# Reordering the opening of a two-layer diffusion trunk: x1 of the fourth token tile, the split of the MLP's first weight unit, and two modulation loads

## The reference

```python
sh_m, sc_m, gt_m, sh_f, sc_f, gt_f = jnp.split((silu_c @ ada_w[i] + ada_b[i])[:, None, :], 6, axis=-1)
h = modulate(rms_norm(x, norm_g[i, 0]), sh_m, sc_m)          # h * (1 + scale) + shift
y = pool_mixer(h, pool_w[j], pool_scale[j])                   # four groups of 256 channels, windows 2, 4, 8, 16
x = x + gt_m * rms_norm(y, norm_g[i, 1])                      # this is x1 below
hf = modulate(rms_norm(x, norm_g[i, 2]), sh_f, sc_f)
x = x + gt_f * rms_norm(jnp.square(jax.nn.relu(hf @ ffn_w1[i])) @ ffn_w2[i], norm_g[i, 3])
```

## Time and profile before

| | us |
|---|---|
| median of three runs | 937.25 |
| lowest, highest | 936.25, 937.87 |
| the profiled execution | 937.82 |
| its span in the profile | 935.8 |
| PE busy in the span | 915.7 |
| ACT busy, DVE busy | 430.9, 648.2 |

### The profile page before, as it was taken

How to read it: one execution, slowest core, us unless ns; L and a number is a source line. 1 busy time by engine, 2 the same in 40 slices (tenths; PEclk the granted TensorE clock), 3 DMA queues, 4 the chain that set the end, 5 groups by cost and what they waited for, 6 DMA issues and landing times.

```text
span 935.8 us, 11417 instructions
## 1 busy us (share of the span) xinstructions
PE 915.7 (98%) x4623; PEld 755.0 (81%) x4623; DVE 648.2 (69%) x625; ACT 430.9 (46%) x523; POOL 48.9 (5%) x80
## 2 busy tenths in 40 slices
PE   8889999999999999999999999999999999999996
PEld 6658888888888888889888888898888888888885
DVE  5696297589678866686667644857857873793688
ACT  6564484454246333264222224555534634543554
POOL 3002110010001001000101000000000000000000
PEclk8999999999999999999999999999999999999998
DMA  9999889527734586324656531183870662175134
GB/s 303 321 352 347 232 221 313 213 74 187 285 114 125 174 314 222 116 76 170 211 179 209 188 124 49 62 298 102 258 260 21 180 202 80 54 217 165 37 68 179
DMA packets 91403, 170.86 MB, mean 183 GB/s; under 512 B 4270, under 2 KB 34066, under 8 KB 91352
## 3 DMA queue, kind: packets, MB, share of 16 engines
q1 hardware_dynamic: 83912, 155.25, 48.5%
q0 software_dynamic: 7440, 14.89, 8.2%
HBM read 163.81 MB, written 6.32 MB: 182 GB/s over the span
## 4 chain that ended last, share of the span: by engine, by line
PE 52%; DVE 2%; issue 1%; ACT 0%; DVEq 0%
PE ps L674 17%; PE ps L676 17%; PE ps L675 17%; PE ps L768 1%; DVE y L1945 0%; DVE y L1580 0%; DVE in_lo L1591 0%; PE ps L703 0%; DVE xs L1956 0%; ACT in_hi L1209 0%; DVE y L1474 0%; DVE y L1586 0%; DVEq L137 0%; DVE y L1543 0%; DVE st L1949 0%
## 5 line engine op out<-in xcount | busy, mean ns | idle before, releaser
L674 PE MATMUL ps<-in_hi,w_parts 128*128 128x512 f32 (+1 forms) x784 | 290.1, 370 | 0.9 <-DVE in_lo L1591 0.5
L675 PE MATMUL ps<-in_lo,w_parts 128*128 128x512 f32 (+1 forms) x784 | 288.1, 367 | 0.0
L676 PE MATMUL ps<-in_hi,w_parts 128*128 128x512 f32 (+1 forms) x784 | 288.1, 367 | 0.0
L1422 DVE TENSOR_TENSOR w_parts<-raw,w_parts 128x2048 fp32r<-128x2048 f32 x81 | 185.6, 2291 | 125.7 <-ACT w_parts L1102 125.6
L1102 ACT ACTIVATE w_parts<-raw 128x2048 fp32r<-128x2048 f32 x81 | 154.8, 1911 | 215.0 <-PE ps L676 201.3
L674 PEld LDWEIGHTS ps<-in_hi,w_parts 128*128 128x128 f32 x784 | 147.8, 188 | 29.4 <-issue 3.3
L676 PEld LDWEIGHTS ps<-in_hi,w_parts 128*128 128x128 f32 x784 | 147.8, 188 | 24.5
L675 PEld LDWEIGHTS ps<-in_lo,w_parts 128*128 128x128 f32 x784 | 147.8, 189 | 24.0
L674 PE MATMUL ps<-w_parts,ops_hi 128*128 128x512 f32 x280 | 109.0, 389 | 0.0
L675 PE MATMUL ps<-w_parts,ops_hi 128*128 128x512 f32 x280 | 108.9, 389 | 0.0
L676 PE MATMUL ps<-w_parts,ops_lo 128*128 128x512 f32 x224 | 87.1, 389 | 0.0
(11 more groups left out here) (202 smaller groups left out, 1037.8 us busy)
## 6 DMA issues: line engine op xcount, KB each, us to landing
raw<-in_ffn_w_dram SPq DMA_DIRECT2D x57, 1024.0 KB, 5.4
ada_raw<-in_ada_w_dram SPq DMA_DIRECT2D x56, 512.0 KB, 6.3
xs<-in_ffn_w_dram SPq DMA_DIRECT2D x14, 1024.0 KB, 5.2
xs<-in_ffn_w_dram POOLq DMA_DIRECT2D x10, 1024.0 KB, 8.6
raw<-in_conv_in_w_dram SPq DMA_DIRECT2D x16, 512.0 KB, 5.3
raw<-in_ada_w_dram SPq DMA_DIRECT2D x4, 1024.0 KB, 10.9
ada_sum<-in_ada_w_dram SPq DMA_DIRECT2D x4, 1024.0 KB, 13.0
win<-in_ada_w_dram SPq DMA_DIRECT2D x4, 1024.0 KB, 12.0
```

The costliest lines, as they stand in the source:

```text
L674: nc.tensor.matmul(o, hi, b_hi, start=start, stop=False, skip_group_check=on)
L675: nc.tensor.matmul(o, hi, b_lo, start=False, stop=False, skip_group_check=on)
L676: return nc.tensor.matmul(o, lo, b_hi, start=False, stop=stop, skip_group_check=on)
L1422: nc.vector.tensor_tensor(w_lo[:, u % W_SLOTS, :], raw_of(u), w_hi[:, u % W_SLOTS, :].bitcast(F32), ALU.subtract).then_inc(w_lo_ready, 1)
```

## The change

In the SP list, pieces 10 and 11 are issued ahead of unit 1. On PE, `start_pairs` has another order of transposes, column work and products: in particular `add_up(PRE_F + 6)` no longer stands between `turn_first(1, 3)` and `turn_first(1, 1)`, and `part(1, 1)` comes before `second_unit(2)`. On ACT, `split_hi(1)` moves behind the root of y, `first_root(3)` ahead of `first_hi(0)`, and `copy_sums(10)` behind `first_hi(2)`. On DVE, `split_lo(1)` moves from ahead of `group_out(3)` to behind `first_x(3)`, which itself moves ahead of `columns(8)`; `first_norm(2)` goes ahead of `first_lo(0)`. No operation is added or removed.

```diff
-        FIRST_TURNED = ((0, 0), (0, 2), (1, 0), (0, 3), (1, 2), (0, 1), (1, 3), (1, 1))
+        FIRST_TURNED = ((0, 0), (0, 2), (1, 0), (0, 3), (0, 1), (1, 2), (1, 3), (1, 1))
...
-            for i in range(2, 10):
+            for i in range(2, PRE_F):
                 load_pre(i)
             load(1)
-            for i in range(10, PRE_F + 6):
+            for i in range(PRE_F, PRE_F + 6):
                 load_pre(i)
             load(2)
...
                 part(0, 0)
+                turn_first(1, 0)
+                turn_up(9)
+                turn_first(0, 3)
                 add_up(PRE_F + 4)
-                turn_first(1, 0)
-                turn_first(0, 3)
+                turn_first(0, 1)
+                turn_first(1, 2)
                 add_up(PRE_F + 5)
-                turn_up(9)
-                turn_first(1, 2)
+                part(1, 0)
                 turn_up(10)
-                turn_first(0, 1)
-                part(1, 0)
                 turn_first(1, 3)
-                add_up(PRE_F + 6)
                 turn_first(1, 1)
                 part(0, 1)
+                add_up(PRE_F + 6)
+                part(1, 1).then_inc(unit_done, 1)
                 add_up(PRE_F + 7)
 
                 pe.wait_ge(f_lo, 4)
                 second_unit(2)
                 turn_up(11)
                 second_unit(3)
-                part(1, 1).then_inc(unit_done, 1)
...
             group_squares(1)
-            split_hi(1)
             group_squares(2)
             group_squares(3)
             act.wait_ge(y0_sum, 2)
             nc.scalar.activation(st0[:, 3, :], st0[:, 2, :], ACT.Sqrt, bias=eps[:, 0:1], scale=1.0 / D).then_inc(y0_rms, 1)
+            split_hi(1)
             first_root(0)
             first_root(1)
             copy_sums(8)
             first_root(2)
+            first_root(3)
             first_hi(0)
             copy_first(0, 2)
-            first_root(3)
             copy_sums(9)
             copy_first(0, 3)
-            copy_sums(10)
             first_hi(1)
+            copy_first(1, 2)
             split_hi(2)
             first_hi(2)
-            copy_first(1, 2)
+            copy_sums(10)
             copy_first(1, 3)
...
             group_gate(0)
-            split_lo(1)
             group_out(3)
...
             first_norm(0)
             first_norm(1)
+            first_x(3)
+            split_lo(1)
             columns(8)
             first_input(0)
+            first_norm(2)
             first_lo(0)
-            first_x(3)
-            first_norm(2)
             first_norm(3)
             first_input(1)
             columns(9)
             first_lo(1)
             first_input(2)
+            first_lo(2)
             split_lo(2)
-            first_lo(2)
+            first_input(3)
+            first_lo(3)
             columns(10)
-            first_input(3)
             first_input(4)
-            first_lo(3)
             first_lo(4)
```

## The result

Over 22 executions each, the changed kernel's median is 940.75 us (938.63 to 943.26) against 937.12 us (935.47 to 938.93) before. The ratio is 1.0037, with a 95% interval of 1.0029 to 1.0046, so 3.5 us slower (2.7 to 4.3); the medians themselves differ by 3.6. The forecast was 941.9, slower, in a range of 938.6 to 943.5.

The account below looks back on a forecast made before the run. PE, almost never idle from 65 to 110 us, was taken as the bound. Waits of 2.6 at part(0, 0) and 0.7 at the transposes plus 1.4 for the clock gave 4.7 us: 941.9 us against the median, range 938.6 to 943.5.

Parts of the forecast that it names:

- PE's fullness behind 65 us: PE almost never idles from 65 to 110 us, so any new wait there comes through to the end.
- Removing the split from 51 us: DVE ahead of group_out(3): x1 and turn_first(0, 0) come 0.46 us sooner, not 2.20; bounds 0 to 0.5 us.
- DVE's queue ahead of part(0, 0): Split and x1 of tile 3 behind the norms: part(0, 0) 2.6 us later, PE stands 3.0 us; bounds 0.9 to 3.5.
- The transposes: turn_first(1, 1) directly after turn_first(1, 3), uncovered: PE waits 0.7 us for ACT's copy; bounds 0.6 to 1.0 us.
- The transfers: Pieces 10 and 11 pass unit 1, the DMA hole fills, pieces 12 on land 1 to 2 us sooner; nothing for PE.
- the predicted sign: In the changed kernel's timeline, add_up(13) on PE would start 1 to 2 us before 61.22.
- The clock: Behind PE's stand at part(0, 0): a fall to half speed costs 1.4 us, between 0 and about 1.7.
- the rival that had a chance of 0.28: Same waits at part(0, 0) and the transposes without the clock's fall: 3.3 us, 940.6 us; chance 0.28.
- the case with 0.50: Main case: PE's stand at part(0, 0) with a fall of the clock, 941.9 us; chance 0.50.
- nothing lies in the stand, so I take a fall: PE's stand before part(0, 0) is longer than either earlier gap and empty, so the clock falls; 1.4 us taken.
- The rule in the prediction, that idleness alone throttles: From the skill's clock gate: throttled is the default and activity releases it, so an idle PE loses its speed.

Follow-up runs that it names:

- POOL's split: Kernel before with the low half of unit 1's split made by POOL instead of DVE: 937.75 us, ratio 1.0000.
- old transfers: Changed kernel with SP's old order alone, unit 1 issued ahead of pieces 10 and 11: 942.16 us, ratio 1.0044.
- cover back: Changed kernel with add_up(18) between the transposes (1, 3) and (1, 1) again: 939.78 us, ratio 1.0024.
- fillers in the stand: Changed kernel with five filler matmuls in the stand before part(0, 0): 939.68 us, ratio 1.0029.
- POOL's split with fillers: Kernel before with fillers before piece 13 and around turn_up(2), and the low half of unit 1's split on POOL: 936.56 us, ratio 0.9986.
- the split alone: Kernel before with both halves of unit 1's split behind the norms of tiles 0 and 1, nothing else changed: 938.59 us, ratio 1.0009.
- the gap filled: Kernel before with six filler matmuls in the 1.95 us in which PE waits for piece 13: 936.29 us, ratio 0.9986.
- the first of the two versions meant to beat both: Kernel before with six fillers before piece 13 and two plus three around turn_up(2): 936.72 us, ratio 0.9988.

## Why the prediction was right

**What bounds.** PE's fullness behind 65 us was the right thing to read: the waits that the change put there came through, 3.4 us by the rows and 3.5 by the ratio. The sum was tested as a whole, with an interval of 2.7 to 4.3; its terms rest on distances in single profiles.

**Removing the split from 51 us.** Forecast 0.46 us for x1, measured 0.45. The changed kernel, and the one with POOL's split, show DVE idle for 1.66 us there.

**DVE's queue ahead of part(0, 0).** Forecast 2.6 us net, that is 7.1 us from norm 1 where it had been 4.06. Measured 7.09 in the changed kernel, and 7.08 or 7.09 in three variants (old transfers, cover back, fillers in the stand). PE was forecast to stand for 3.0 us; the idle row says 0.77, 1.11, 1.58 or 2.17, depending on how late PE itself was. The idle row of the waiting engine understates the wait when that engine is slow ahead of it. The distance on the engine waited for does not.

**The transposes.** Forecast 0.7 us, measured 0.78 as idle time and 0.83 in PE's progress. Undoing it brought 1.0 us in PE's progress, and 1.3 us in time within overlapping intervals.

**The transfers.** Forecast nothing for PE, with pieces 12 on landing 1 to 2 us sooner. The hole closed, but piece 13 did not come sooner: PE still waited 1.94 us for it, and started on it 8.33 us after the end of the last pooling product (50.30 to 58.63) where it had been 8.46 (52.76 to 61.22). That `add_up(13)` lies 2.6 us before 61.22 looks like the predicted sign and is the lead of 2.46 us. Pieces 12 and 13 wait for `d_lo`, the last pooling operand, and the hole lay ahead of that. "Worth nothing" held in the profiled executions, where the distance is 7.09 us with old and new transfers. The run with the old transfers was too spread to exclude a microsecond, and the profile of POOL's split with fillers shows piece 11 binding x1 in the old order, so the new transfers may keep x1's gain where PE is early. No run tests that in the changed kernel.

**The clock.** This is the term that was mis-sized. I took 1.4 us for a fall behind the stand as the likeliest case, and its forecast was 941.9; the sum without it, 3.3 us and 940.6, is what the medians show (940.75). So the point forecast was too high by a term, and the measured time lies at the rival that had a chance of 0.28, not at the case with 0.50. What failed is the step "nothing lies in the stand, so I take a fall". In three of the four profiled executions with an idle stand and no filler (0.77 us in the changed kernel, 1.58 with the cover back, 1.76 with the split alone) the clock stayed at 1.00 behind it; in the fourth (2.17 us) it fell to 0.66 over 5 us. The size was near: that fall cost 1.50 us, 1.4 was taken. It was the odds that were too high. I had also priced falls as if only the change brought them. The kernel before has its own, as the earlier trace rows showed between 36 and 40 us, and with the gap filled it is 1.3 us faster by the ratio, 0.7 between the medians. The changed kernel does not pay for a fall at 58 to 65 us, because DVE's queue is longer there, and the old order does; this should make the difference of the two a little smaller than the waits alone, which no run separates. Whether the fall behind the stand explains the changed kernel's times of 942 and over stays open: no profile shows such an execution of the changed kernel itself, and the filler in the stand didn't clearly remove them. The mean granted clock of the seven slowest executions (0.991 in three, 0.992 to 0.995 in four) against that of the other fifteen (0.992 to 0.997) doesn't settle it.

The Trainium skill (TensorE: Matmul & The Clock Gate, Part 1: The HAM clock gate) says that it is run-variable how many matmuls of one kernel pass before its clock turns up. The runs agree that the place is not fixed, here for falls: between versions that are the same ahead of 42 us, the fall lay at 28 to 33, at 36 to 40, or at 43 to 47 us. The rule in the prediction, that idleness alone throttles, is too simple for this kernel.

## What to carry to other kernels

Before a piece of work is moved off a chain, look for the chain's next predecessor: here moving 2.20 us of work gained only 0.45 us, because the product it waited for was nearly as late. Then price its new place by the whole in-order queue behind it, up to the first instruction that the full engine waits for, and check whether a transfer or product that is moved was covering a copy between two users of one bank. Where a small difference is read from single profiles, compare distances between two instructions of one chain, and list the stretches of low clock first.

## What was not expected of the hardware

Falls of TensorE's clock sat at different places in almost every profile of the first 75 us, also in versions that are alike ahead of them: from 9 to 16 (before), 36 to 40, 43 to 47, 28 to 33, 58 to 65 us. The run with the filled stand and the first of the two versions meant to beat both have none. Ahead of one the engine was partly idle (0.65 of 2.00 us busy), but greater idleness (0.27 of 2.00 us busy) passed without one in the same execution. A fall of 3.4 us early in the chain cost x1 1.52 us; one of 7 us beside DVE's longer chain left the distance at 7.09 us.

POOL subtracts 128 x 2048 in 4.59 us where DVE needs 2.28, and DVE's instructions beside it kept their durations (1.22 us for `group_out(3)` with and without).
